# One channel tile of a 31-tap depthwise convolution moved from GpSimd to VectorE

## What is computed

```
q, k, v, f, a, gate = split(x @ w_in)            # one projection, 1024 -> 2568
o_c = fox(q, k, v, logf)                          # prompt: 8 heads, 4 query blocks of 128; sample: paged cache
u   = a * sigmoid(gate)                           # (tokens, 512)
y_d[t, c] = sum_j ext[t + j, c] * conv_w[j, c]    # 31 taps, causal: ext = 30 earlier rows, then u
y_d = silu(layernorm(y_d + conv_b))
out = concat([o_c, y_d]) @ w_out
```

## Time and profile before

| | |
|---|---|
| median of three runs | 1560.31 us |
| span of the profiled execution | 1557.5 us |
| outside the span (median less span) | 2.8 us |
| TensorE busy | 1436.6 us, 92% |
| VectorE busy | 522.2 us, 34% |
| ScalarE busy | 482.3 us, 31% |
| GpSimd busy | 681.7 us, 44% |
| mean granted TensorE clock | 0.946 of full speed |

### The profile page before, as it was taken

One profiled execution on the slowest core, in us unless ns is written; L12 is line 12 of the kernel. 1 busy time (PEld: TensorE's weight loads), 2 busy tenths in 40 slices (PEclk: granted clock), 3 DMA queues, 4 the chain that ended last, 5 costly groups with the idle time before them and its releaser, 6 DMA issues.

```text
span 1557.5 us, 30210 instructions
## 1 busy us (share of the span) xinstructions
PE 1436.6 (92%) x11701; PEld 1301.2 (84%) x11701; DVE 522.2 (34%) x688; ACT 482.3 (31%) x622; POOL 681.7 (44%) x356
## 2 busy tenths in 40 slices
PE   7999899799999999997999788897969999999995
PEld 5999769699999999996799633445959999999995
DVE  2343843810000000146311388787460000000035
ACT  2431212443344321233211321234253344332123
POOL 2433302655555454454232289400555555454451
PEclk9999879899999999998999966899989999999998
DMA  5222211222333332221889954881213222333211
GB/s 213 81 81 82 69 32 42 69 70 71 110 97 96 99 113 93 81 72 44 261 293 336 338 151 135 199 267 61 82 42 95 83 92 94 94 99 109 93 38 55
DMA packets 88020, 180.30 MB, mean 116 GB/s; under 512 B 30025, under 2 KB 30042, under 8 KB 87442
## 3 DMA queue, kind: packets, MB, share of 16 engines
q1 hardware_dynamic: 87202, 175.46, 35.2%
q0 software_dynamic: 752, 3.92, 1.1%
HBM read 173.29 MB, written 6.05 MB: 115 GB/s over the span
## 4 chain that ended last, share of the span: by engine, by line
PE 75%; DVE 13%; issue 5%; ACT 2%; SPq 2%; POOL 1%; DMA 1%; DVEq 0%; ACTq 0%; POOLq 0%
PE ps L853 62%; DVE pj L1746 2%; DVE x L1359 2%; PE ps L1206 1%; PE ps L1207 1%; DVE rstd L1334 1%; PE ps L1236 1%; POOL wl L699 1%; SPq L332 1%; PE ps L1225 1%; DVE x L1348 1%; PE ps L1041 1%; PE ps L1158 1%; DVE rstd L1356 1%; PE ps L973 1%
## 5 line engine op out<-in xcount | busy, mean ns | idle before, releaser
L699 POOL TENSOR_TENSOR wl<-raw,wh 128x1024 fp32r<-128x1024 f32 (+1 forms) x180 | 460.9, 2561 | 744.4 <-ACT wh L386 744.4
L853 PE MATMUL ps<-xh,wh 128*128 128x260 f32 x2368 | 487.2, 287 | 57.6 <-POOL xl L764 36.6
L853 PE MATMUL ps<-xh,wl 128*128 128x260 f32 x2368 | 479.6, 284 | 0.0
L853 PE MATMUL ps<-xl,wh 128*128 128x260 f32 x2368 | 479.2, 284 | 0.0
L386 ACT ACTIVATE wh<-raw 128x1024 fp32r<-128x1024 f32 (+1 forms) x180 | 201.1, 1117 | 763.3 <-PE ps L853 757.8
L853 PEld LDWEIGHTS ps<-xh,wh 128*128 128x128 f32 x2368 | 367.7, 190 | 73.1 <-issue 41.4
L853 PEld LDWEIGHTS ps<-xh,wl 128*128 128x128 f32 x2368 | 367.8, 190 | 0.0
L853 PEld LDWEIGHTS ps<-xl,wh 128*128 128x128 f32 x2368 | 367.4, 190 | 0.0
L1400 DVE TENSOR_TENSOR hid_t<-ps,gate_t 128x520 f32<-128x520 f32 x44 | 30.8, 700 | 476.7 <-PE ps L853 476.7
L853 PE MATMUL ps<-hh,wh 128*128 128x260 f32 x704 | 142.3, 283 | 0.0
L853 PE MATMUL ps<-hh,wl 128*128 128x260 f32 x704 | 141.6, 282 | 0.0
(11 more groups left out here) (280 smaller groups left out, 1293.8 us busy)
## 6 DMA issues: line engine op xcount, KB each, us to landing
raw<-in_w_f_in SPq DMA_DIRECT2D x88, 512.0 KB, 3.5
pages<-in_cache_kt SPq DMA_DIRECT2D x128, 256.0 KB, 4.1
pages<-in_cache_v SPq DMA_DIRECT2D x128, 256.0 KB, 3.9
raw<-in_w_f_out SPq DMA_DIRECT2D x32, 704.0 KB, 4.1
raw<-in_w_ab_in SPq DMA_DIRECT2D x24, 512.0 KB, 3.6
raw<-in_w_cd_in SPq DMA_DIRECT2D x20, 512.0 KB, 4.4
raw<-in_w_ab_out SPq DMA_DIRECT2D x8, 512.0 KB, 3.5
raw<-in_w_cd_out SPq DMA_DIRECT2D x8, 512.0 KB, 5.5
```

What stands on the lines that cost most here:

```text
L699: nc.gpsimd.tensor_tensor(wl[:, j % SPLIT, 0:b * P], raw[:, j, 0:b * P], wh[:, j % SPLIT, 0:b * P].bitcast(F32), ALU.subtract).then_inc(w_ ...
L853: mm = nc.tensor.matmul(out[h], w[:, slot, block_at * P:block_at * P + P], rows[:, k, HT * h:HT * h + HT], start=start and a, stop=stop and z)
```

## The change

VectorE folds all four tiles: tap 0 becomes four TENSOR_SCALAR and each of the 30 unit slots has four taps in place of three. GpSimd's 61 instructions on the fourth tile and the scratch tile are gone, and so are the semaphores `tap_product` and `pool_tap` with the waits on them (GpSimd's own before L818, and TensorE's before L949). Nothing takes the scratch tile's place in memory and no other tile moves. GpSimd's sample convolution now follows `u_ready` and the load of `ext_d` directly.

```diff
-DVE_TILES = 3
+DVE_TILES = 4
...
-        tap_t = at("tap_t", [P, 4 - DVE_TILES, TP], small[0])
...
             pool.wait_ge(u_ready, 1)
             wd = par_of("conv_d", 4 * CF_TAPS).rearrange("p (t j) -> p t j", j=CF_TAPS)
-            POOL_TILES = 4 - DVE_TILES
-            for t in range(DVE_TILES, 4):
-                nc.gpsimd.tensor_scalar(pj2[:, CD_GATE + t, 0:TP], upad[:, t, 0:TP], wd[:, t, 0:1],
-                                        par_of("cf_b", 4)[:, t:t + 1], ALU.mult, ALU.add)\
-                    .then_inc(pool_tap, 1)
-            with pool.Fori(1, CF_TAPS) as j:
-                pool.wait_ge(pool_tap, j * POOL_TILES)
-                for t in range(DVE_TILES, 4):
-                    nc.gpsimd.tensor_tensor(tap_t[:, t - DVE_TILES, :], upad[:, t, bass.ds(j, TP)],
-                                            wd[:, t, bass.ds(j, 1)].to_broadcast([P, TP]), ALU.mult).then_inc(tap_product, 1)
-                pool.wait_ge(tap_product, j * POOL_TILES)
-                for t in range(DVE_TILES, 4):
-                    nc.gpsimd.tensor_tensor(pj2[:, CD_GATE + t, 0:TP], pj2[:, CD_GATE + t, 0:TP], tap_t[:, t - DVE_TILES, :],
-                                            ALU.add).then_inc(pool_tap, 1)
 
             U = CD_GATE
             pool.wait_ge(conv_d_in, 16)
-            pool.wait_ge(pool_tap, CF_TAPS * POOL_TILES)
             nc.gpsimd.tensor_copy(ext_d[:, :, :, CF_TAPS - 1], pj2[:, U:U + 4, TP:T]).then_inc(d_sampled, 1)
...
                 pe.wait_ge(d_tap, CF_TAPS * DVE_TILES)
-                pe.wait_ge(pool_tap, CF_TAPS * (4 - DVE_TILES))
```

More of the change, by code:

```diff
@@ L255, in bass_hybrid_step @@
             sem(n) for n in ("s_ready_all", "m_turned", "m_diag", "m_cast", "s_shifted", "p_all", "l_part", "l_sum", "pv_all", "self_cast"))
-        d_sig, u_ready, d_tap, tap_product, pool_tap, d_sampled, y_cd = (sem(n) for n in ("d_sig", "u_ready", "d_tap", "tap_product", "pool_tap", "d_sampled", "y_cd"))
+        d_sig, u_ready, d_tap, d_sampled, y_cd = (sem(n) for n in ("d_sig", "u_ready", "d_tap", "d_sampled", "y_cd"))
         block = ctx.enter_context(nc.Block())
```

## The result

The changed kernel takes 1532.49 us (median of four runs, 1531.21 to 1536.6) against 1560.28 for the kernel before: a ratio of 0.9824, 95% interval 0.9805 to 0.9843. The forecast was 1532.5. Its profiled execution has a span of 1530.2 us, 27.3 less than before.

A forecast was written before the change was run, and what follows sets the result against it. Bound: GpSimd's activity lengthens VectorE's first-pass taps, and TensorE pays in waits and a lower clock. -0.9 - 29.6 + 2.0 + 0.66 = -27.8, span 1529.7, plus 2.8 outside: 1532.5 us; range 1526 to 1544.

The forecast's parts named there:

- Tap price: VectorE's fourth tap in each unit adds 0.66 us, the undisturbed distance between tap starts; upper bound 1.34.
- Before the loop: Tap 0 as four TENSOR_SCALAR without GpSimd beside them takes 1.68 us instead of 2.58: -0.9 us.
- The moved sample steps: GpSimd's L818 to L833 run from 900.2 to about 910.5 us; cost to VectorE 0 to 1 us, taken as 0.
- First pass: First pass of the attention loop, scores to unit 15's scaling: 61.62 (second pass as template) + 2.79 + 2.0 = 66.4 us, against 96.04.
- The late clock: First pass reached with a cold TensorE: unit 3's scores 12.29 us after unit 0's, against 9.50 in the second pass; adds 2.79.
- the lag: Fourth tap delays what TensorE awaits from VectorE: 0.30 us per four-unit group, 2.0 us a pass; bounds 0 and 10.
- Second pass: Second pass of the attention loop loses 2.0 us to the fourth tap.
- Tail: Behind the loop, the last taps, which L949 awaits, cost another 0.66 us.
- The late pages: Rival: the `out_conv_d_s` write, 16.0 us to land, delays first-pass page loads; with 8 us of it, 1540 us; chance 0.12.
- The clock rival: TensorE held up in every unit, first pass keeps clock 0.70 and takes about 91 us: 1551 us; chance 0.05.
- The slower rival: First pass's 1341 ns taps come from something else in that pass, not GpSimd: 1584.6 us; chance 0.03.
- The signs named: Right: 120 taps near 745 ns, passes near 72 and 68 us, clock near 1.00 from 913. Wrong: L1236 page waits.

The follow-up runs named there:

- idle chain: Changed kernel with GpSimd again running a chain of products and additions of the same shapes, into unused scratch: 1577.38 us, ratio 1.0098 to the kernel before.

## Why the prediction was right, step by step

- *The bound.* The first pass was long because GpSimd's chain lengthened VectorE's taps, and TensorE paid for that twice. The idle chain shows the first half by itself (1490 ns beside it, 747 without).
- *Tap price 0.66 us.* Four taps from start to end take 2.73 us against 2.07 for three: 0.66.
- *Before the loop, -0.9.* Tap 0 takes 1.92 us for four tiles where 1.68 was estimated: -0.66 against the 2.58 before. The loop's first scores come 1.29 earlier (900.71 to 899.42); the other 0.63 was there before `u`.
- *The moved sample steps, 0.* They ran from 900.07 to 909.79, as worked out. They held the pass's first scaling for 3.27 us; in the kernel before they held one for 3.76 us at 985.54. In the run in which that scaling took 0.68, unit 3's scores came 9.33 us behind unit 0's against 9.89, so the price is some 0.6 at most, as far as the clock's own differences let it be told, within the 0 to 1 us given.
- *First pass, 66.4 us.* It took 65.11 (899.42 to 964.53), by terms that missed in both directions. The late clock was given 2.79 and cost 0.39 (9.89 against 9.50). The page wait was given nothing and cost 1.44. The rest, 1.66, is the lag, given as 2.0.
- *Between the passes, 5.68 unchanged.* 5.68 (964.53 to 970.21).
- *Second pass, +2.0.* It took 4.06 more (65.68 against 61.62): 1.93 of lag, as worked out, and 2.13 because the clock came up later in this pass than in the template (11.63 against 9.50). This term was not in the sum. The same matmuls in the other runs of the changed kernel and its edits took 8.50 to 11.63 us for the stretch in this pass, and 9.33 to 13.35 in the first, so it differs by 3 to 4 us for no reason that these runs show, which the range covered.
- *Tail, +0.66.* From the last scaling to the layer norm's first subtraction 7.42 became 8.09: 0.67.
- *Sum.* -1.29 - 30.93 + 4.06 + 0.67 and 0.19 behind the loop make -27.30, the difference of the spans. The forecast was -27.8. That it came within 0.5 us is partly luck: the two clock terms, -2.4 and +2.1, nearly cancel.
- *The rivals.* The late pages were real and small: the write landed near 917, pages took up to 12.5 us, and unit 4 waited once; moving the write away removed the wait. The argument that the write would have landed by the time of the first reload overlooked the pages issued while it was under way: the first reload went out from 905.53 us on and took 10.8 to 12.5, so it landed behind the write, and unit 4's matmul started at 919.78. The clock rival did not come about even with five taps (0.91 and 0.93 in the two passes). The slower rival fell with the idle chain.
- *The signs named.* Taps, passes, TensorE's wait for L1737 and GpSimd's silence came as named. Two did not. A wait of L1236 (now L1219) on pages stood among the signs of being wrong and came, at 1.44 us, and pages issued from 920 to 930 us still took up to 7.4. And the clock was not near 1.00 from 913 us on: it was 1.00 from 907.5 to 970 and fell to 0.50 (972.5 to 980) at the start of the second pass, where the kernel before has 0.50 as well (1002.5 to 1007.5).

Not settled: what decides when the clock comes up within a pass, and what makes some executions 3 us longer ahead of the stage.

## What to carry to other kernels

Before giving GpSimd a share of VectorE's elementwise work, look at what VectorE's instructions of the same stretch last beside it and without it: here a quarter of the taps moved away made the other three quarters 1.8 times as long. Where TensorE waits on such an engine, count the matmuls' own time as well as the wait: three quarters of the first pass's gain came from the clock. And when work is added to an engine that others wait for, its place among the units costs more than its sum: the same 120 taps cost 0.3 to 0.5 us a group in one order and nothing in another.

## What the runs showed of the hardware beyond that

- A GpSimd that only writes leaves VectorE's taps, with two tensor inputs, alone (742 ns) and holds its TENSOR_SCALAR, with one: 0.77 to 0.83 us against 0.29 to 0.49.
- One small scaling took 3.27 us where it takes 0.29 alone: it began at 902.10, while GpSimd issued the write of `conv_d_s`, and ended at 905.37, with GpSimd's product (902.95 + 2.33 = 905.28). In the runs with that write issued elsewhere it took 0.68 and 0.37, and ended with the product as well.
- A write of 480 KB that takes 15.8 us to land stretches the landing of 256 KB pages issued beside it, from 899 to 920 us: 8.3 to 12.5 us in the changed kernel, at most 4.4 and 5.0 in the two runs that send it behind the loop.
